# Routing gates of a decoder trunk placed by float32r products of eight columns, as a rounded part and a remainder

## The chip, the cores and the metric

The kernel runs on one core of a Trainium2 chip. A core has the engines TensorE (PE in the profile: matrix products; PEld is its weight load), VectorE (DVE), ScalarE (ACT), GpSimd (POOL) and SyncE (SP, whose queue starts most of the transfers). The metric is the time of one execution in microseconds; it is 798.51 for the kernel before.

## What is computed

The reference is a decoder trunk of two layers over 256 tokens of 1024 numbers in float32. Each layer mixes tokens with three kinds of attention, attends to 256 memory tokens, and ends in a mixture of 16 experts in 4 groups. The change touches only the last. Its gates are, for each token, a weight for two experts of one group:

```python
scores = sigmoid(x @ router_w);  biased = scores + router_bias
g_sel  = argmax over the 4 groups of (sum of the two highest biased scores in the group)
expert_idx = the two highest biased in group g_sel
w = scores[expert_idx];  w = w / sum(w)          # gates, zero for all other experts
hg = x @ w_gate[e];  hu = x @ w_up[e]            # for each expert e: 1024 -> 256
a  = silu(hg) * hu * gates[:, e]
out += a @ w_down[e]                             # 256 -> 1024
```

## The kernel before

**Arithmetic.** Large products are made of halves: each float32 operand is kept as a part rounded to float32r and a remainder, and one product is three float32r products (`product`, L1669 to L1671). ScalarE makes the rounded part of each weight piece (L564), VectorE the remainder (`split_lo`, L570), into a ring of four slots. A piece is 128 partitions by 1024 columns; an expert has four pieces for its gate and up matrices (names `U<e>`) and two for its down matrix (`D<e>`).

**The experts.** Every token goes to one group. Its place in the group's list of up to 128 slots is kept as a matrix `sel` of zeros and ones (tokens by slots, for each of two token tiles `t` and four groups `g`), of type float32r. `gather` multiplies the tokens by `sel`, so that each group's tokens stand in slots (`xg_hi`, `xg_lo`). The 16 experts then run one after another, each on the 128 slots of its group: `experts_up` (four pieces of six products), an activation (`silu` on ScalarE, `act_of` on VectorE, L1390, which also multiplies by the gate `gs[:, e]` of each slot), two transposes (`turn_a`, L1939), and `experts_down`.

**The gates.** On VectorE, `router_first` and `router_gates` work out two weights per token in a row of small operations on the 4 experts of the token's group. Each ends in a semaphore, and the next waits for it (`step`). The last one, L1370, writes `g4`, tokens by the 4 experts of the group, in float32. On TensorE, `place_gates` (L2008 to L2014) brings them to the slots: for each group and token tile, `sel` is the stationary operand and `g4` the moving one, 8 products of 4 columns into columns 0 to 15 of `bank[5]`. VectorE copies them out into `gs` (L1617).

**What sets the order.** Each engine's order is written out by hand. On VectorE it is, after the piece u+4: `router_first`, `router_gates`, `full_group` (three small operations, L1380 to L1385, about groups with more than 128 tokens), the remainders of pieces u+5 and u+6, a wait for `gs_done`, L1617, `act_of` for expert 0, then pieces u+7 and u+8. On TensorE it is, in `expert_turn(l, 0)`: `experts_up` of expert 1 for piece 0 (u+4), `place_gates`, `experts_up` for piece 1 (u+5), `turn_a` of expert 0 (which waits for `act_of`), pieces 2 and 3, and `experts_down` of expert 0. All of this happens once in each of the two layers.

Of the kernel before, what the change touches and what calls it, by code (L numbers as in the profile page):

```python
# [19 lines left out]
F32 = mybir.dt.float32  # L20
F32R = mybir.dt.float32r
I32 = mybir.dt.int32
ALU = mybir.AluOpType
ACT = mybir.ActivationFunctionType
AX = mybir.AxisListType.X

P = 128
# [5 lines left out]
NE, NG, EPG, DE = 16, 4, 4, 256  # L33
# [43 lines left out]
def build(nc, x, mem, positions, w_in, b_forget, mla_q_gain, mla_kv_gain, mla_w_uq, mla_w_ukv, w_mix_out,  # L77
          ln_mix_g, ln_mix_b, xattn_w_q, xattn_w_kv, xattn_w_o, ln_mem_g, ln_mem_b, router_w, router_bias,
          expert_w_gate, expert_w_up, expert_w_down, ln_ffn_g, ln_ffn_b, out):
    _, T, DM = x.shape  # L80
    L = w_in.shape[0]
    TT = T // P
# [60 lines left out]
    with ExitStack() as ctx:  # L143
# [3 lines left out]
        def sb(name, shape, dt=F32, at=None):  # L147
            size = int(np.prod(shape[1:])) * 4
            size = -(-size // 64) * 64
            if at is None:  # L150
                at = place[0]
                place[0] += size
            return nc.alloc_sbuf_tensor_at(name, shape, dt, offset=at), at + size


        raw, _ = sb("raw", [P, RAW, 1024])
        w_split, _ = sb("w_split", [P, 2, SPL, 1024], F32R)
        w_hi, w_lo = w_split[:, 0, :, :], w_split[:, 1, :, :]
        xs, _ = sb("xs", [P, TT, DM])
        xT_at = place[0]  # L160
        xT_hi, _ = sb("xT_hi", [P, KC, T], F32R)
        xT_lo, _ = sb("xT_lo", [P, KC, T], F32R)
        memT_hi, _ = sb("memT_hi", [P, KC, T], F32R)
        memT_lo, _ = sb("memT_lo", [P, KC, T], F32R)
        gb, _ = sb("gb", [P, 2, DM])
        ident, _ = sb("ident", [P, P])

        causal, _ = sb("causal", [P, 2 * P])
        dilmask, _ = sb("dilmask", [P, 2 * P])
        dilcount, _ = sb("dilcount", [P, 2 * P])  # L170
        upto, _ = sb("upto", [P, P], F32R)
# [18 lines left out]
        iota, _ = sb("iota", [P, P])  # L190
        ing_r, _ = sb("ing", [P, TT * NG], F32R)
        ing = ing_r[:, :].bitcast(F32)
        g4, _ = sb("g4", [P, TT, EPG])
        posg, _ = sb("posg", [P, TT, NG])
        pos1, _ = sb("pos1", [P, TT])
        gs, _ = sb("gs", [P, NE])
# [94 lines left out]
        def signal(name, per, ahead=0):  # L291
            return Signal(sem(name), per, ahead)
# [86 lines left out]
        fz_a = signal("fz_a", 2)  # L379
        aug = signal("aug", 2)  # L380
        rope_step = signal("rope_step", 26)
        route = signal("route", 29)
        group_at = 14
        counted_over = signal("counted_over", 3)
        xs_a = signal("xs_a", TT)
# [687 lines left out]
        def _(dve):  # L1073
# [210 lines left out]
            def by_tile(v, n_):  # L1284
                return v[:, 0:TT * n_].rearrange("p (t n) -> p t n", t=TT)
# [71 lines left out]
            def router_gates(l):  # L1357

                step = stepper(l)
                mine, other = by_tile(R[13], EPG).unsqueeze(3).to_broadcast(GRID), by_tile(R[13], EPG).unsqueeze(2).to_broadcast(GRID)  # L1360
                over_, tied, rank = R[4], R[5], G4(R[6])
                step(nc.vector.tensor_tensor(grid(over_), other, mine, ALU.is_gt))
                step(nc.vector.tensor_tensor(grid(tied), other, mine, ALU.is_equal))
                step(nc.vector.tensor_tensor(grid(tied), grid(tied), earlier[:, :, :].unsqueeze(1).to_broadcast(GRID), ALU.mult))
                step(nc.vector.tensor_tensor(over_, over_, tied, ALU.add))
                step(nc.vector.tensor_reduce(by_tile(rank, EPG), grid(over_), AX, ALU.add))
                step(nc.vector.scalar_tensor_tensor(G4(R[7]), rank, 1.5, G4(R[14]), ALU.is_lt, ALU.mult))
                step(nc.vector.tensor_reduce(R[9][:, 0:TT], by_tile(R[7], EPG), AX, ALU.add))
                step(nc.vector.reciprocal(R[9][:, TT:2 * TT], R[9][:, 0:TT]))
                step(nc.vector.tensor_tensor(g4[:, :, :], by_tile(R[7], EPG),  # L1370
                                             R[9][:, TT:2 * TT].unsqueeze(2).to_broadcast([P, TT, EPG]), ALU.mult))
                assert q[0] == route.per, q[0]

            def over_full(l):
# [72 lines left out]
            for l in range(L):  # L1447
# [166 lines left out]
                split_lo(dve, u + 5)  # L1614
                split_lo(dve, u + 6)
                dve.wait_ge(gs_done.sem, gs_done.at(l, 1))
                nc.vector.tensor_copy(gs[:, :], bank[5][:, 0:NE]).then_inc(gs_ready.sem, 1)  # L1617
                dve.wait_ge(gs_ready.sem, gs_ready.at(l, 1))
                act_of(l, 0, 0)
                for i in range(u + 7, u + 9):  # L1620
# [30 lines left out]
        def _(pe):  # L1651
# [39 lines left out]
            def by_tile(l):  # L1691

                open_job(l, "A")
                parts = {}
                for t, b in enumerate(banks(l, "A")):
                    last_half = evac_v[l][job[f"XT{t}"]]
                    pe.wait_ge(job_v.sem, job_v.at(l, last_half - 1))
                    for j in range(4):
                        if t == 0:
                            if j == 2:  # L1700
                                pe.wait_ge(x_in[1], 16)
                                turn_x(l, "XT1", 1, 0)
                            parts[j] = sub_in(index[l, "A", j])
                        if j == 2:
                            pe.wait_ge(job_v.sem, job_v.at(l, last_half))
                        for k in range(2):
                            lhs = tuple(v[:, 2 * j + k, t * P:(t + 1) * P] for v in xT)
                            r = tuple(v[:, k * A_W:(k + 1) * A_W] for v in parts[j])
                            ins = product(b[:, 0:A_W], lhs, r, j == 0 and k == 0, j == 3 and k == 1)
                        if t == TT - 1:  # L1710
                            ins.then_inc(split_free, 1)
# [294 lines left out]
            def place_gates(l):  # L2006

                pe.wait_ge(route.sem, route.at(l, route.per))  # L2008
                for g in range(NG):
                    for t in range(TT):  # L2010
                        ins = nc.tensor.matmul(bank[5][:, g * EPG:(g + 1) * EPG],
                                               sel[:, t, g * P:(g + 1) * P].bitcast(F32), g4[:, t, :],
                                               start=g == 0 and t == 0, stop=g == NG - 1 and t == 1, skip_group_check=True)
                ins.then_inc(gs_done.sem, 1)  # L2014

# [36 lines left out]
            def further_tokens(l):  # L2052
                pe.wait_ge(y_v.sem, y_v.at(l, 2 * NG))
                pe.wait_ge(ov_picked.sem, ov_picked.at(l, 1 + TT))
                pe.nop().then_inc(paused_t, 1)
                for t in range(TT):
                    nc.tensor.transpose(bank[6][:, t * P:(t + 1) * P], ov_sel[:, t, :], ident[:, :])
                for t in range(TT):
                    nc.tensor.matmul(bank[7][:, 0:EPG], ov_sel[:, t, :], g4[:, t, :], start=t == 0, stop=t == 1)
                for f in range(KC):  # L2060
                    for t in range(TT):
                        ins = nc.tensor.matmul(bank[4 + f // 4][:, (f % 4) * P:(f % 4 + 1) * P],
                                               xs[:, t, f * P:(f + 1) * P], ov_sel[:, t, :],
                                               start=f % 4 == 0 and t == 0, stop=t == 1, skip_group_check=True)
                ins.then_inc(ov_gathered.sem, 1)
                pe.wait_ge(ov_kept.sem, ov_kept.at(l, 5))
                pe.nop().then_inc(paused_t, 1)
                with pe.Fori(0, EPG) as e:
                    pe.wait_ge(ov_in[l], e * 48 + 48)
                    for kc in range(KC):  # L2070
                        ins = nc.tensor.matmul(bank[6][:, :], ov_x[:, kc, :], ov_up[:, kc, :], start=kc == 0, stop=kc == KC - 1)
                    ins.then_inc(ov_upped.sem, 1)
                    pe.wait_ge(ov_act.sem, ov_act.at(l, e + 1))
                    for c_ in range(2):
                        ins = nc.tensor.transpose(bank[7][:, c_ * P:(c_ + 1) * P], act_a[:, 0, c_ * P:(c_ + 1) * P], ident[:, :])
                    ins.then_inc(ov_turned.sem, 1)
                    pe.wait_ge(ov_aT_in.sem, ov_aT_in.at(l, e + 1))
                    for c_ in range(2):
                        for h in range(2):
                            ins = nc.tensor.matmul(bank[4 + h][:, :], ov_aT[:, c_, :], ov_down[:, c_, 512 * h:512 * h + 512],  # L2080
                                                   start=c_ == 0, stop=c_ == 1)
                    ins.then_inc(ov_used.sem, 1)
                pe.wait_ge(ov_y_in.sem, ov_y_in.at(l, ov_y_in.per))
                pe.nop().then_inc(paused_t, 1)
                for t in range(TT):
                    for h in range(2):
                        nc.tensor.matmul(bank[2 * t + h][:, :], ov_selT[:, t * P:(t + 1) * P],
                                         ov_y[:, 512 * h:512 * h + 512], start=False, stop=False, skip_group_check=True)
# [203 lines left out]
```

## Time and profile before

| | |
|---|---|
| median of three runs | 798.51 us (797.60 to 798.68) |
| the profiled execution | 800.22 us, its span 798.6 us |
| TensorE matmul busy | 783.0 us, 98% of the span |
| VectorE busy | 620.9 us, 78% |
| ScalarE busy | 512.0 us, 64% |
| mean granted TensorE clock | 0.996 of full |
| transfers | 177.06 MB, 222 GB/s over the span |

The span is the profiled stretch on the core; the execution's own time is 1.62 us longer. Busy time says how long an engine had work, not whether the kernel waited for it; the timeline shows where an engine sat idle and which instruction ended that. In the timeline a row's second number is how long its instructions took from first start to last end, `x16` how many were merged into it, and the brackets hold the idle time before it and what released it. A float32 product stands in the records as two matmuls and two weight loads, so the 8 products of `place_gates` are `x16`; a float32r product stands as one, though its type is printed as f32 too.

### The profile page before, as it was taken

The numbers are of one execution on the slowest core, as the hardware profiler recorded it, in microseconds if no ns is written. First come the engines' busy times: TensorE is split into PE (matmuls) and PEld (weight loads), VectorE is DVE, ScalarE is ACT, GpSimd is POOL, SyncE is SP. The second block draws the span as 40 slices with busy tenths as digits, with TensorE's granted clock in tenths as the row PEclk, the third lists the DMA queues.
The fourth block names the chain that finished last, engine by engine and source line by source line (L and its number), as shares of the span: only waits on it lengthen the run. The fifth ranks groups of instructions, "written<-read, shape, count | busy, mean of one in ns | idle before, by whom it ended". The sixth has DMA issues, their size and how long they took to land.

```text
span 798.6 us, 11973 instructions
## 1 busy us (share of the span) xinstructions
PE 783.0 (98%) x4307; PEld 676.7 (85%) x4307; DVE 620.9 (78%) x1066; ACT 512.0 (64%) x794; POOL 79.3 (10%) x150
## 2 busy tenths in 40 slices
PE   7999999999999999999999999999999999999995
PEld 7999997789888888888899998878998788888884
DVE  4767867685669999999884578777655899999995
ACT  4755556454547788888755566565443768888873
POOL 3259100020000000000011233002000000000000
PEclk9999999999999999999999999999999999999998
DMA  9965343564345699999956544445633359999951
GB/s 326 319 201 177 135 134 124 164 234 142 106 150 164 225 365 369 367 364 368 361 142 205 157 159 132 133 158 185 199 112 116 133 168 359 368 364 367 368 192 54
DMA packets 123118, 177.06 MB, mean 222 GB/s; under 512 B 10176, under 2 KB 92624, under 8 KB 123056
## 3 DMA queue, kind: packets, MB, share of 16 engines
q1 hardware_dynamic: 121072, 169.56, 63.6%
q0 software_dynamic: 1984, 6.70, 2.8%
q8 instruction: 36, 0.59, 0.3%
q14 instruction: 26, 0.21, 0.1%
HBM read 175.18 MB, written 1.05 MB: 221 GB/s over the span
## 4 chain that ended last, share of the span: by engine, by line
PE 88%; DVE 8%; issue 1%; ACT 1%; DMA 1%; DVEq 0%; SPq 0%; ACTq 0%
PE bank L1669 24%; PE bank L1671 24%; PE bank L1670 24%; DVE w_split L570 2%; PE bank L1876 2%; PE bank L1919 2%; PE bank L1910 2%; PE bank L1889 2%; DVE xg_lo L1605 1%; PE bank L1845 1%; PE bank L1865 1%; PE bank L1939 1%; PE bank L1782 1%; DVE xs L1208 1%; PE bank L2024 1%
## 5 line engine op out<-in xcount | busy, mean ns | idle before, releaser
L570 DVE TENSOR_TENSOR w_split<-raw,w_split 128x1024 fp32r<-128x1024 f32 (+3 forms) x334 | 385.4, 1176 | 93.3 <-ACT w_split L564 88.6
L564 ACT ACTIVATE w_split<-raw 128x1024 fp32r<-128x1024 f32 (+3 forms) x334 | 334.8, 1010 | 108.5 <-PE bank L1671 95.1
L1669 PE MATMUL bank<-w_split,xg_hi 128*128 128x512 f32 x256 | 103.0, 402 | 0.1
L1671 PE MATMUL bank<-w_split,xg_lo 128*128 128x512 f32 x256 | 100.2, 391 | 0.0
L1670 PE MATMUL bank<-w_split,xg_hi 128*128 128x512 f32 x256 | 99.9, 390 | 0.0
L1669 PE MATMUL bank<-w_split,xT_hi 128*128 128x384 f32 (+2 forms) x224 | 78.6, 351 | 1.9 <-DVE xT_lo L1135 1.9
L1671 PE MATMUL bank<-w_split,xT_lo 128*128 128x384 f32 (+2 forms) x224 | 76.5, 342 | 0.0
L1670 PE MATMUL bank<-w_split,xT_hi 128*128 128x384 f32 (+2 forms) x224 | 76.4, 341 | 0.0
L1671 PEld LDWEIGHTS bank<-w_split,xg_lo 128*128 128x128 f32 x256 | 48.0, 188 | 10.3
L1669 PEld LDWEIGHTS bank<-w_split,xg_hi 128*128 128x128 f32 x256 | 48.1, 188 | 9.6 <-DVE xg_lo L1605 0.6
L1670 PEld LDWEIGHTS bank<-w_split,xg_hi 128*128 128x128 f32 x256 | 48.2, 188 | 9.0
L1669 PE MATMUL bank<-w_split,mixT_hi 128*128 128x512 f32 x128 | 51.8, 405 | 0.1
L1671 PE MATMUL bank<-w_split,mixT_lo 128*128 128x512 f32 x128 | 50.0, 391 | 0.0
L1670 PE MATMUL bank<-w_split,mixT_hi 128*128 128x512 f32 x128 | 50.0, 390 | 0.0
L1671 PE MATMUL bank<-w_split,aT_lo 128*128 128x512 f32 x128 | 49.8, 389 | 0.0
L1669 PE MATMUL bank<-w_split,aT_hi 128*128 128x512 f32 x128 | 49.8, 389 | 0.0
L1670 PE MATMUL bank<-w_split,aT_hi 128*128 128x512 f32 x128 | 49.8, 389 | 0.0
L1669 PEld LDWEIGHTS bank<-w_split,xT_hi 128*128 128x128 f32 x224 | 42.6, 190 | 2.7 <-DVE xT_lo L1135 2.3
L1670 PEld LDWEIGHTS bank<-w_split,xT_hi 128*128 128x128 f32 x224 | 42.8, 191 | 0.2
L1671 PEld LDWEIGHTS bank<-w_split,xT_lo 128*128 128x128 f32 x224 | 42.6, 190 | 0.1
L794 ACT ACTIVATE qkT<-bank 66x512 f32<-66x512 f32 (+2 forms) x26 | 15.5, 596 | 33.2 <-PE bank L1845 27.0
L1669 PE MATMUL bank<-xT_hi,w_split 128*128 128x256 f32 x112 | 32.4, 289 | 0.0
(325 smaller groups left out, 1514.3 us busy)
## 6 DMA issues: line engine op xcount, KB each, us to landing
raw<-in_expert_w_gate_dram SPq DMA_DIRECT2D x128, 256.0 KB, 6.0
raw<-in_expert_w_up_dram SPq DMA_DIRECT2D x128, 256.0 KB, 7.6
raw<-in_expert_w_down_dram SPq DMA_DIRECT2D x64, 512.0 KB, 7.8
raw<-in_xattn_w_kv_dram SPq DMA_DIRECT2D x32, 512.0 KB, 3.7
raw<-in_w_in_dram SPq DMA_DIRECT2D x40, 384.0 KB, 4.9
raw<-in_w_mix_out_dram SPq DMA_DIRECT2D x16, 512.0 KB, 3.4
raw<-in_xattn_w_q_dram SPq DMA_DIRECT2D x16, 512.0 KB, 3.4
raw<-in_xattn_w_o_dram SPq DMA_DIRECT2D x16, 512.0 KB, 5.2
```

Source lines behind the costliest of these rows:

```text
L564: nc.scalar.activation(halves_of(i)[0][:, 0:w], raw[:, i % RAW, 0:w], ACT.Copy).then_inc(hi_ready, 1)
L570: nc.vector.tensor_tensor(lo[:, 0:w], raw[:, i % RAW, 0:w], hi[:, 0:w].bitcast(F32), ALU.subtract).then_inc(lo_ready, 1)
L794: nc.scalar.activation(qkT[0:d, qk_slot(h), :], B_QK[0:d, :], ACT.Copy).then_inc(qkT_ready.sem, n)
L1208: nc.vector.scalar_tensor_tensor(half, half, ALPHA, product, ALU.mult, ALU.add, accum_out=st[:, 2 * n_ + t, 2 * h:2 * h + 1]).then_inc(sig ...
L1605: nc.vector.tensor_tensor(xg_lo[:, f, :, :].rearrange("p g s -> p (g s)"), bank[XG_BANKS[f]][:, :], xg_hi[:, f, :, :].rearrange("p g s -> ...
L1669: nc.tensor.matmul(o, lhs[0], rhs[0], start=first, stop=False, skip_group_check=shared)
L1670: nc.tensor.matmul(o, lhs[0], rhs[1], start=False, stop=False, skip_group_check=shared)
L1671: return nc.tensor.matmul(o, lhs[1], rhs[0], start=False, stop=last, skip_group_check=shared)
L1876: ins = nc.tensor.matmul(o[:, t * T:(t + 1) * T], qTx[:, 2 * g + c_, t * P:(t + 1) * P], kTx[:, 2 * g + c_, :], start=c_ == 0, stop=c_ == 1)
L1889: ins = nc.tensor.transpose(B_PT[:, k * P:(k + 1) * P], pr[:, k * P:(k + 1) * P], ident[:, :])
L1910: ins = nc.tensor.matmul(B_O[k * HD:(k + 1) * HD, q0:T], v[:, t, g - 1 + k, :], turned_of(h - 1 + k)[:, t * T:t * P + T], start=t == 0, st ...
L1919: ins = nc.tensor.matmul(value_bank(h)[:, dblk * T:(dblk + 1) * T], vx[:, c_, f * P:(f + 1) * P], turned_of(h)[:, c_ * T:(c_ + 1) * T], st ...
```

## The change

`g4` becomes `g_parts` of type float32r, with two halves for each tile: the gates rounded to float32r, and what the rounding left out. L1370 writes the first half, and a new step of two operations (one for each token tile, with the reciprocal as a per-partition scalar) works out the product again and subtracts the first half from it. `place_gates` multiplies by both halves at once: 8 products of 8 columns, both operands float32r, into columns 0 to 31 of `bank[5]`. On the way out a sum over pairs replaces the copy. `route` counts 31 instead of 29 steps. The rest of the diff is in `further_tokens`, a branch that is taken only where a group has more than 128 tokens.

```diff
-        g4, _ = sb("g4", [P, TT, EPG])
+        g_parts, _ = sb("g_parts", [P, TT, 2, EPG], F32R)
...
-        route = signal("route", 29)
+        route = signal("route", 31)
...
-                step(nc.vector.tensor_tensor(g4[:, :, :], by_tile(R[7], EPG),
+                step(nc.vector.tensor_tensor(g_parts[:, :, 0, :], by_tile(R[7], EPG),
                                              R[9][:, TT:2 * TT].unsqueeze(2).to_broadcast([P, TT, EPG]), ALU.mult))
+                step(*(nc.vector.scalar_tensor_tensor(g_parts[:, t, 1, :], by_tile(R[7], EPG)[:, t, :],
+                                                      R[9][:, TT + t:TT + t + 1], g_parts[:, t, 0, :].bitcast(F32),
+                                                      ALU.mult, ALU.subtract) for t in range(TT)))
...
                 dve.wait_ge(gs_done.sem, gs_done.at(l, 1))
-                nc.vector.tensor_copy(gs[:, :], bank[5][:, 0:NE]).then_inc(gs_ready.sem, 1)
+                nc.vector.tensor_reduce(gs[:, :].rearrange("p (g e) -> p g e", g=NG),
+                                        bank[5][:, 0:2 * NE].rearrange("p (g s e) -> p g e s", g=NG, s=2), AX, ALU.add)\
+                    .then_inc(gs_ready.sem, 1)
...
-                        ins = nc.tensor.matmul(bank[5][:, g * EPG:(g + 1) * EPG],
-                                               sel[:, t, g * P:(g + 1) * P].bitcast(F32), g4[:, t, :],
+                        ins = nc.tensor.matmul(bank[5][:, 2 * g * EPG:2 * (g + 1) * EPG],
+                                               sel[:, t, g * P:(g + 1) * P], g_parts[:, t, :, :].rearrange("p s e -> p (s e)"),
                                                start=g == 0 and t == 0, stop=g == NG - 1 and t == 1, skip_group_check=True)
```

The order on VectorE from the end of the router's steps to the first activation, before. `rt` is the router's scratch, `g_82` is `g4`, `fl` belongs to `full_group`, and `w_split` is the ring of weight pieces (here u+5 and u+6).

```order
L1369 RECIPROCAL rt<-rt 128x2
L1370 TENSOR_TENSOR g_82<-rt 128x8
L1380 SCALAR_TENSOR_TENSOR fl<-iota,fl 128x4
L1382 TENSOR_REDUCE fl<-fl 128x2
L1385 CAST flag<-fl 1x2
L570 TENSOR_TENSOR w_split<-raw,w_split 128x1024 x2
L1617 COPY gs<-bank 128x16
L1390 SCALAR_TENSOR_TENSOR act_a<-silu,gs,bank 128x256
```

The same place in the changed kernel.

```order
L1369 RECIPROCAL rt<-rt 128x2
L1370 TENSOR_TENSOR g_parts<-rt 128x2x4
L1372 SCALAR_TENSOR_TENSOR g_parts<-rt,g_parts 128x4 x2
L1383 SCALAR_TENSOR_TENSOR fl<-iota,fl 128x4
L1385 TENSOR_REDUCE fl<-fl 128x2
L1388 CAST flag<-fl 1x2
L570 TENSOR_TENSOR w_split<-raw,w_split 128x1024 x2
L1620 TENSOR_REDUCE gs<-bank 128x16
L1393 SCALAR_TENSOR_TENSOR act_a<-silu,gs,bank 128x256
```

Two operations are new, in front of `full_group` and the two weight pieces, and the copy has become a reduction; nothing else on this engine has moved.

On TensorE, before: the last products of expert 1's piece 0, `place_gates`, and the first of its piece 1.

```order
L1670 MATMUL bank<-w_split,xg_hi 128x512
L1671 MATMUL bank<-w_split,xg_lo 128x512
L2011 MATMUL bank<-g_82,sel 128x4 x8
L1669 MATMUL bank<-w_split,xg_hi 128x512
L1670 MATMUL bank<-w_split,xg_hi 128x512
```

The same place in the changed kernel.

```order
L1675 MATMUL bank<-w_split,xg_hi 128x512
L1676 MATMUL bank<-w_split,xg_lo 128x512
L2016 MATMUL bank<-g_parts,sel 128x8 x8
L1674 MATMUL bank<-w_split,xg_hi 128x512
L1675 MATMUL bank<-w_split,xg_hi 128x512
```

The eight products stay where they were; their moving operand has eight columns in place of four.

## Rows read from the trace of the kernel before

**Rows 1.** The page: the chain that ended last, by engine.
```profile
PE 88%; DVE 8%; issue 1%; ACT 1%; DMA 1%; DVEq 0%; SPq 0%; ACTq 0%
```

**Rows 2.** Timeline, VectorE, layer 0: start us, us, engine, line, work [idle before <-releaser].
```profile
265.17 0.17 DVE L1370 TENSOR_TENSOR g<-rt 128x8 f32<-128x8 f32 x1
265.61 0.16 DVE L1380 SCALAR_TENSOR_TENSOR fl<-iota,fl 128x4 f32<-128x4 f32 x1 [0.27 <-DVE g L1370]
...
266.07 0.16 DVE L1385 CAST flag<-fl 1x2 int32<-1x2 f32 x1
266.15 2.34 DVE L570 TENSOR_TENSOR w_split<-raw,w_split 128x1024 fp32r<-128x1024 f32 x2
268.42 0.15 DVE L1617 COPY gs<-bank 128x16 f32<-128x16 f32 x1
268.61 0.48 DVE L1390 SCALAR_TENSOR_TENSOR act_a<-silu,gs,bank 128x256 f32<-128x256 f32 x1
```

**Rows 3.** Timeline, TensorE's weight loads in the same stretch of layer 0.
```profile
265.39 1.86 PEld L2011 LDWEIGHTS bank<-g,sel 128*128 128x128 f32 x16 [0.23 <-DVE g L1370]
267.41 0.19 PEld L1669 LDWEIGHTS bank<-w_split,xg_hi 128*128 128x128 f32 x1 [0.16 <-DVE w_split L570]
...
269.14 0.20 PEld L1939 LDWEIGHTS bank<-ident,act_a 128*128 128x128 f32 x2 [0.51 <-DVE act_a L1390]
```

**Rows 4.** Timeline, the same place in layer 1: VectorE.
```profile
651.24 0.17 DVE L1370 TENSOR_TENSOR g<-rt 128x8 f32<-128x8 f32 x1
651.44 0.16 DVE L1380 SCALAR_TENSOR_TENSOR fl<-iota,fl 128x4 f32<-128x4 f32 x1
...
654.44 0.48 DVE L1390 SCALAR_TENSOR_TENSOR act_a<-silu,gs,bank 128x256 f32<-128x256 f32 x1
```

**Rows 5.** Timeline, the same place in layer 1: TensorE's weight loads.
```profile
651.45 1.86 PEld L2011 LDWEIGHTS bank<-g,sel 128*128 128x128 f32 x16 [0.22 <-DVE g L1370]
653.24 0.19 PEld L1669 LDWEIGHTS bank<-w_split,xg_hi 128*128 128x128 f32 x1
...
654.97 0.20 PEld L1939 LDWEIGHTS bank<-ident,act_a 128*128 128x128 f32 x2 [0.51 <-DVE act_a L1390]
```

**Rows 6.** Stage table: us, busy time (instructions) of each engine, granted clock, DMA.
```profile
core 0: us, PE busy (x) PEld busy (x) DVE busy (x) ACT busy (x) POOL busy (x), PEclk, DMA share, GB/s
265.39:269.34 3.95, 3.80 (x26) 3.11 (x25) 3.56 (x8) 1.35 (x2) 0.00 (x0) 1.00 0.36 103
269.34:300.00 30.66, 30.66 (x140) 25.24 (x139) 29.30 (x30) 25.12 (x29) 0.00 (x0) 1.00 1.04 349
788.00:792.00 4.00, 1.28 (x6) 0.74 (x4) 3.77 (x13) 1.63 (x4) 0.00 (x0) 1.00 0.00 0
792.00:796.00 4.00, 0.00 (x0) 0.00 (x0) 3.93 (x5) 1.45 (x3) 0.00 (x0) 0.60 0.32 131
```

**Rows 7.** Timeline, VectorE, an earlier place where two small operations share one wait.
```profile
247.06 0.17 DVE L1319 TENSOR_TENSOR rt<-rt 128x16 f32<-128x16 f32 x1
247.16 0.17 DVE L1320 TENSOR_TENSOR rt<-rt 128x16 f32<-128x16 f32 x1
247.36 0.17 DVE L1321 TENSOR_TENSOR rt<-rt 128x8 f32<-128x8 f32 x1
```

**Rows 8.** VectorE operations by line: count, ns min/median/max, first to last start.
```profile
L1355 DVE TENSOR_REDUCE rt<-rt x4: 209/210/211, 262.7 to 649.3; 128x8 f32<-128x32 f32 x4
...
L1366 DVE TENSOR_REDUCE rt<-rt x2: 186/186/186, 264.3 to 650.4; 128x8 f32<-128x32 f32 x2
...
L1214 DVE TENSOR_SCALAR st<-st x12: 214/214/214, 163.6 to 791.7; 128x1 f32<-128x1 f32 x12
```

**Rows 9.** Timeline, TensorE: the ranking products, with float32r operands and four columns.
```profile
248.86 0.27 PE L1975 MATMUL bank<-ing,upto 128*128 128x4 f32 x1 [0.27 <-DVE ing L1330]
...
249.21 0.36 PE L1980 MATMUL bank<-ing,ones 128*128 128x4 f32 x2
249.44 0.48 PE L1812 MATMUL bank<-memT_hi,ones 128*128 128x512 f32 x1
```

More of the change, by code:

```diff
@@ L2058, in further_tokens @@
                 for t in range(TT):
-                    nc.tensor.matmul(bank[7][:, 0:EPG], ov_sel[:, t, :], g4[:, t, :], start=t == 0, stop=t == 1)
+                    for s_ in range(2):
+                        nc.tensor.matmul(bank[7][:, 0:EPG], ov_sel[:, t, :], g_parts[:, t, s_, :].bitcast(F32),
+                                         start=t == 0 and s_ == 0, stop=t == 1 and s_ == 1)
                 for f in range(KC):
```

## Prediction

> **What bounds the kernel now.** I read the chain that ended last first: 88% of it lies on TensorE and 8% on VectorE [rows 1]. So time taken off TensorE is worth something wherever TensorE is not waiting, and time put on VectorE costs nothing wherever VectorE is ahead. The question is which of the two holds at the one place per layer that is edited. For that I read the timeline of both engines around line 1370, in each layer.
>
> In layer 0 VectorE ends the gates at 265.17 + 0.17 = 265.34, and TensorE's first weight load of the placing starts at 265.39, after 0.23 us in which it sat idle for L1370 [rows 2, 3]. The reader is to see that TensorE is already the one that waits. The placing's 16 loads take 1.86 us. The next product, of piece u+5, starts at 267.41; the bracket gives 0.16 us of idle time and names the remainder L570 as what ended it [rows 3]. VectorE did that remainder right behind `full_group`: two in a row from 266.15, 2.34 us for both, so the first ends at about 267.3 [rows 2]. Then VectorE goes on without a gap: second remainder, copy of the gates at 268.42, activation at 268.61 for 0.48 us. TensorE's transposes start at 269.14 after 0.51 us of waiting for that activation [rows 2, 3].
>
> So between 265.17 and 269.14 every start on VectorE follows from its own instruction before, and TensorE waits for it three times. The copy never waited for the products: the placing ends before 267.41, and the copy stands in VectorE's queue at 268.42 behind the two remainders. Layer 1 is the same to a few hundredths: 0.22 us of waiting at the placing, the activation at 654.44, 0.51 us of waiting at 654.97 [rows 4, 5]. Only at piece u+5 no idle time is shown there: at 653.24 placing and remainder end together [rows 5].
>
> Behind this place it is the other way round. From 269.34 to 300 TensorE is busy 30.66 of 30.66 us and VectorE 29.30 [rows 6]. A TensorE that starts that stretch later ends it later; nothing there takes a delay back. Transfers are not tied to the clock on the wall either: their buffers come free by these same engines, so they move along.
>
> **The change, part by part.**
>
> First, two operations on VectorE in front of `full_group`. They share one wait. Where two small operations already do that, the first starts at 247.06, the second at 247.16 and the next step at 247.36: such a step is 0.30 us long [rows 7]. A step of one is 0.20 us, L1370 to L1380 in layer 1 [rows 4]. The new step is added whole, so +0.30 us in front of `full_group`, of both remainders, the copy and the activation, and also in front of the placing, which now waits for 31 steps. Below, it can't be less than one step, 0.20 us. Above: the new operations take a scalar from each partition, and a tiny operation that does (L1214) is recorded at 0.214 us against some 0.16 to 0.17 for those without [rows 8, 2]; with that and no overlap within the pair it is 0.21 + 0.25 = 0.46 us. I take 0.30, since the pair is the nearest row.
>
> The Trainium skill says on this, in "VectorE: DVE Perf Modes", section "Terms", that the pipe is drained after each operation and that the next can't issue before. Read strictly, the pair would stand end to end, 0.17 + 0.20 = 0.37 us; by that the sum below would be 0.8 in place of 0.7. The trace doesn't bear the strict reading out: the second starts 0.10 us after the first, whose record is 0.17 long [rows 7].
>
> Second, the reduction in place of the copy. The copy is 0.15 us [rows 2]. Reductions that read 32 numbers per partition take 0.186 us with the summed ones side by side and 0.210 us with a stride of four [rows 8]; the new one reads 32 with a stride of four, from `bank[5]`, and writes 16. I take +0.04 us; the bounds are 0 and, since no row has a reduction out of a bank, twice the larger difference, 0.11 us. It stands straight in front of the activation, so all of it is on the path.
>
> Third, the placing on TensorE. The records have 16 loads in 1.86 us; with 0.19 for one load that is 1.67/15 = 0.11 us from start to start [rows 3]. Products with float32r operands are one load and one matmul each, and go at the same pace: five of them from 248.86 to 249.44, 0.116 us each [rows 9]. That they have four columns and the new ones eight hardly counts, because the load sets the pace. So the placing shrinks from about 1.86 to 8 x 0.116 = 0.93 us, 0.93 us less per layer. Its worth: TensorE would be done at 265.69 + 0.93 = 266.62, but the remainder of u+5 now comes at 267.41 + 0.30 = 267.71. The idle 0.16 us becomes 1.09 us. The saving turns into waiting and buys nothing; nor does the earlier `gs_done`, since VectorE gets to it only at 268.72.
>
> Then nothing else is late: the transposes start at 269.14 + 0.34 = 269.48, still behind the activation, with about the same 0.5 us of waiting, since the products of u+5 and the activation are both moved by 0.30 and 0.34 us. The transposed remainders, pieces u+7 to u+9 and the products after them keep their distances.
>
> Sum per layer: 0.30 + 0.04 = 0.34 us. Two layers: +0.68 us. The span goes from 798.6 to 799.3, the profiled execution from 800.22 to 800.9. The median of the runs lies 1.71 us under that execution; with the same distance it goes from 798.51 to 799.2 us.
>
> One thing can shift this by tenths. In layer 0 VectorE starts L1380 0.44 us after L1370, in layer 1 0.20 us [rows 2, 4]; the extra 0.24 us has no cause in the profile. A program with other instructions in front of that place may have such a pause in neither layer or in both: -0.24 or +0.24. With it, the bounds of the sum are 2 x 0.20 - 0.24 = 0.2 us and 2 x (0.46 + 0.11) + 0.24 = 1.4 us, so 798.7 to 799.9, and with the spread of the runs shown (0.9 below the median to 0.2 above) 797.8 to 800.1.
>
> **The rivals.**
>
> *TensorE is what ends the stretch.* Then halving the placing pays. For it: the chain is 88% TensorE [rows 1], and in layer 1 the profile shows no idle time in front of 653.24 [rows 5]. Against it: in both layers TensorE waits 0.51 us for the activation afterwards, and would wait longer if it came earlier. If all of it paid and VectorE's part were hidden, 2 x 0.93 = 1.9 us less: 796.7 us. If the saving paid and the additions too counted, 1.2 us less: 797.3, which can't be told from no change.
>
> *The additions are hidden.* If a later place had room for 0.34 us, the time would stay at 798.5. For it, TensorE waits for VectorE, ScalarE and transposed tiles here and there outside the experts. Against it, each of these waits hangs on work that moves along with the delay.
>
> *The clock falls.* This one is slower. The wait in front of u+5 grows to 1.1 us, with another 0.5 us only 1.5 us later. If that made the granted clock fall to 1.2 GHz for the products behind it, they would take twice as long. An expert is 36 products and two transposes; at 30.66/140 = 0.22 us each [rows 6] that is 8.3 us. For half an expert at the lower level I put 4.2 us: one layer gives 803.4 us, both 807.6. It decides if any stretch behind 267 or 653 shows less than 1.00. Against it stands the end of the program: from 788 to 792 TensorE is busy 1.28 of 4 us and the clock is still 1.00; it reads 0.60 only in the next four, in which TensorE does nothing [rows 6]. The Trainium skill warns of this in "TensorE: Matmul & The Clock Gate", section "Why this matters for your kernels": idle gaps between bursts of matmuls bring the clock back to the half rate. As far as these rows show it, a gap of 1.1 us among busy microseconds is not such a gap.
>
> *The change doesn't do what it says.* If the eight-column products were run in two passes like float32 ones, the placing would stay at 1.9 us and end at 265.69 + 1.86 = 267.55, still before 267.71. The time would be the forecast's, 799.2; only the reason for the missing gain would differ.
>
> **How the numbers follow.** The forecast, +0.7 us with its bounds and with the case of two passes inside it, gets 0.76. Hidden additions 0.12, TensorE as the bound 0.07 (half of it at 796.7), a falling clock 0.05. About 0.2%, 1.6 us, is what a measurement of this kernel can tell from no change: below 796.9 is faster, above 800.1 slower. Faster comes from the rival at 796.7 alone, 0.04. Slower is the falling clock and a little of the forecast's upper bound, 0.08. The rest, 0.88, is no change. The range is 797.4 to 800.4 us.
>
> **What the changed profile would show.** The placing as eight loads in about 0.9 us. Idle time of 1 us or more on TensorE in front of the next L1669's counterpart, ended by the remainder. From the start of L1370 to the start of the first activation 3.78 us in layer 0, where it was 3.44, and 3.54 in layer 1, where it was 3.20. A wait near 0.5 us in front of the transposes. Clock 1.00 throughout. The forecast is wrong if TensorE's wait for the activation shrinks well below 0.5 us or is gone, which would mean that VectorE was not what ended the stretch, or if the added step measures far from 0.30 us.

## The result and the profile after

The changed kernel takes 799.82 us (799.28 to 800.91, 18 runs) against 798.69 (797.40 to 800.17, 18 runs) for the one before. The ratio is 1.0017, interval 1.0010 to 1.0024: 0.8 to 1.9 us slower. The ratio lies inside the 0.2% that the prediction calls no change, the upper end of its interval just outside. The same comparison made again (same_after, below) gave 1.0024 (1.0014 to 1.0034). The forecast was +0.7 us, so direction and class were right and 799.82 lies in the range of 797.4 to 800.4; the size was about half of what was measured.

The chain that ended last, on the page of the profile after, has one hundredth more of VectorE than [rows 1]:

```profile
PE 88%; DVE 9%; issue 1%; ACT 1%; DMA 1%; DVEq 0%; SPq 0%; ACTq 0%
```

VectorE in layer 0, from the timeline, against [rows 2]:

```profile
263.70 0.17 DVE L1370 TENSOR_TENSOR g_parts<-rt 128x8 fp32r<-128x8 f32 x1
263.91 0.36 DVE L1372 SCALAR_TENSOR_TENSOR g_parts<-rt,g_parts 128x4 fp32r<-128x4 f32 x2
264.30 0.16 DVE L1383 SCALAR_TENSOR_TENSOR fl<-iota,fl 128x4 f32<-128x4 f32 x1
...
264.83 2.34 DVE L570 TENSOR_TENSOR w_split<-raw,w_split 128x1024 fp32r<-128x1024 f32 x2
267.10 0.17 DVE L1620 TENSOR_REDUCE gs<-bank 128x16 f32<-128x32 f32 x1
267.31 0.48 DVE L1393 SCALAR_TENSOR_TENSOR act_a<-silu,gs,bank 128x256 f32<-128x256 f32 x1
```

TensorE's weight loads there, against [rows 3]:

```profile
264.32 0.97 PEld L2016 LDWEIGHTS bank<-g_parts,sel 128*128 128x128 f32 x8 [0.61 <-DVE g_parts L1372]
266.09 0.19 PEld L1674 LDWEIGHTS bank<-w_split,xg_hi 128*128 128x128 f32 x1 [0.81 <-DVE w_split L570]
...
267.85 0.20 PEld L1944 LDWEIGHTS bank<-ident,act_a 128*128 128x128 f32 x2 [0.53 <-DVE act_a L1393]
```

And layer 1, against [rows 4, 5], first VectorE, then the weight loads:

```profile
649.93 0.17 DVE L1370 TENSOR_TENSOR g_parts<-rt 128x8 fp32r<-128x8 f32 x1
...
650.52 0.16 DVE L1383 SCALAR_TENSOR_TENSOR fl<-iota,fl 128x4 f32<-128x4 f32 x1
...
653.53 0.48 DVE L1393 SCALAR_TENSOR_TENSOR act_a<-silu,gs,bank 128x256 f32<-128x256 f32 x1
```

```profile
652.32 0.19 PEld L1674 LDWEIGHTS bank<-w_split,xg_hi 128*128 128x128 f32 x1 [0.81 <-DVE w_split L570]
```

What to see: the placing halves, 1.86 to 0.97 us, and TensorE then waits 0.81 us for the remainder of piece u+5, where it waited 0.16 or not at all. (The prediction had 1 us or more here for layer 0; the pause of 0.24 us, which went, makes up most of the difference.) The transposes still wait 0.53 us. From L1370 to the activation it is 3.61 us in layer 0 (3.44 before, 3.78 forecast) and 3.60 in layer 1 (3.20 before, 3.54 forecast). From there on the two profiles agree: activation 0 to L1370 of layer 1 is 382.62 us against 382.63, the activation of layer 1 to the last entry of the chain 141.03 against 141.01. So this profile holds +0.57 us. Its span is still 0.9 us shorter than the span before, because it reached L1370 1.47 us sooner; and the starts of profiles differ by up to 2.8 us from one to another (below). Comparing two spans would have given the wrong sign.

### The profile page after: what moved, and what is told of

Same layout as the page of the kernel before. It is cut to its first block, busy times and chain, and to the rows that moved or that the text cites. A ratio compares the mean times of both kernels' runs of the same rounds, so it can differ in the third digit from the quotient of the medians.

```text
span 797.7 us, 11945 instructions
## 1 busy us (share of the span) xinstructions
PE 780.1 (98%) x4291; PEld 673.5 (84%) x4291; DVE 621.6 (78%) x1070; ACT 511.7 (64%) x794; POOL 79.4 (10%) x150
## 3 DMA queue, kind: packets, MB, share of 16 engines
HBM read 175.18 MB, written 1.05 MB: 221 GB/s over the span
## 4 chain that ended last, share of the span: by engine, by line
PE 88%; DVE 9%; issue 1%; ACT 1%; DMA 1%; DVEq 0%; SPq 0%; ACTq 0%
PE bank L1674 24%; PE bank L1676 24%; PE bank L1675 24%; DVE w_split L570 2%; PE bank L1881 2%; PE bank L1924 2%; PE bank L1915 2%; PE bank L1894 2%; DVE xg_lo L1608 1%; PE bank L1850 1%; PE bank L1870 1%; PE bank L1944 1%; DVE xs L1208 1%; PE bank L1787 1%; PE bank L2029 1%
```

## The experiments

All were timed beside the kernel before, whose median was 798.6 to 798.8 us each time. Three stretches of each profile, in us, from starts on VectorE and the start of the chain's last entry:

| | L1370 to activation, layer 0 | the same, layer 1 | activation of layer 1 to the chain's last entry | time, ratio (interval) |
|---|---|---|---|---|
| same_before | 3.44 | 3.20 | 141.01 | 798.62, 1.0003 (0.9994 to 1.0011) |
| same_after | 3.61 | 3.60 | 142.31 | 800.40, 1.0024 (1.0014 to 1.0034) |
| tensor_part | 3.44 | 3.20 | 141.01 | 798.61, 1.0002 (0.9993 to 1.0011) |
| vector_part | 3.59 | 3.59 | 143.23 | 805.85, 1.0097 (1.0082 to 1.0111) |
| vector_part_b | 3.59 | 3.59 | 141.00 | 799.54, 1.0014 (1.0004 to 1.0024) |
| after_placed_twice | 3.61 | 3.61 | 142.38 | 799.63, 1.0014 (1.0005 to 1.0023) |
| after_wide_filler | 3.61 | 3.61 | 141.01 | 799.24, 1.0001 (0.9992 to 1.0010) |
| late_before | 2.91 | 2.67 | 141.45 | 798.18, 0.9994 (0.9985 to 1.0003) |
| late_after | 3.09 | 3.08 | 141.04 | 798.56, 0.9997 (0.9988 to 1.0006) |
| moved_64 | 3.44 | 3.20 | 143.19 | 805.10, 1.0080 (1.0067 to 1.0092) |
| reordered_before | 2.60 | 2.58 | 140.97 | 799.22, 1.0005 (0.9996 to 1.0014) |
| reordered_after | 1.95 | 1.96 | 140.79 | 797.71, 0.9984 (0.9975 to 0.9992) |

L1354 first started at 262.5 us in the first profile before, at 259.8 in tensor_part's and at 259.7 in after_placed_twice's: that is how far the starts differ. In the two reordered kernels one remainder has moved in front of L1370, so their first two columns can't be held against the other rows; the text on them uses another start.

**same_before and same_after: the two kernels again.**

> The kernel before, unchanged, against itself: what a comparison of this kernel with no change gives, and how far two profiles of it lie apart. All theories: ratio 1.000 within 0.1%. From the start of L1370 to the activation 3.2 us in layer 1; in layer 0 3.44 us if the pause of 0.24 us is fixed to this program, 3.20 us if it comes and goes by itself.

The pause of 0.24 us in layer 0 is in every profile that keeps this order without the step (and in late_before), and in none with the step: it belongs to the program, not to chance.

> The changed kernel again, on the same chip as the parts. Theory A: the sum of the two parts, +0.6 to +0.8 us, ratio 1.001; both layers 3.6 us from L1370 to the activation. If the 1.3 us measured before hold here while vector_part gives 0.7 and tensor_part 0, something other than the two parts costs 0.6 us.

Slower than the parts allow. The activation is where it should be, but the stretch behind it is 1.3 us longer, 142.31. Its timeline, TensorE:

```profile
654.28 0.78 PE L1674 MATMUL bank<-w_split,xg_hi 128*128 128x512 f32 x1
654.85 0.63 PE L1675 MATMUL bank<-w_split,xg_hi 128*128 128x512 f32 x1
655.28 0.63 PE L1676 MATMUL bank<-w_split,xg_lo 128*128 128x512 f32 x1
655.71 0.63 PE L1674 MATMUL bank<-w_split,xg_hi 128*128 128x512 f32 x1
656.13 0.63 PE L1675 MATMUL bank<-w_split,xg_hi 128*128 128x512 f32 x1
656.56 0.52 PE L1676 MATMUL bank<-w_split,xg_lo 128*128 128x512 f32 x1
656.92 0.40 PE L1674 MATMUL bank<-w_split,xg_hi 128*128 128x512 f32 x1
657.15 0.40 PE L1675 MATMUL bank<-w_split,xg_hi 128*128 128x512 f32 x1
```

A product every 0.43 us in place of 0.23: the lower of the two clock levels. Its stage table says the same (the third figure from the end is the granted clock, as a share of full; half is the lower level):

```profile
650.00:660.00 10.00, 9.09 (x37) 7.03 (x37) 8.99 (x15) 4.91 (x7) 0.00 (x0) 0.83 0.67 211
```

Another fall of this kind stands near the start of most profiles, whatever the kernel. The stage from 9 to 13 us in same_before, then in same_after:

```profile
9.00:13.00 4.00, 4.00 (x16) 3.29 (x15) 2.62 (x3) 1.69 (x2) 0.00 (x0) 0.57 1.05 396
9.00:13.00 4.00, 4.00 (x20) 3.82 (x19) 2.71 (x3) 1.33 (x2) 0.00 (x0) 1.00 1.06 398
```

Nine of the fourteen profiles show it, between 8 and 15 us; before, tensor_part, late_before, same_after and after_placed_twice don't. This matters below.

**tensor_part: only the placing in one pass.** The gates are rounded to float32r and the remainder is left out of the computation.

```diff
-        g4, _ = sb("g4", [P, TT, EPG])
+        g4, _ = sb("g4", [P, TT, EPG], F32R)
...
-                                               sel[:, t, g * P:(g + 1) * P].bitcast(F32), g4[:, t, :],
+                                               sel[:, t, g * P:(g + 1) * P], g4[:, t, :],
```

> The kernel before, with only the placing in one pass: the gates are rounded to float32r and the remainder is left out of the computation, 8 products of 4 columns, copy as before. Theory A: TensorE is free 0.9 us earlier and waits as much longer for the remainder of piece u+5 (about 0.9 to 1.0 us of idle time in layer 0, 0.8 in layer 1); time +0.0 us, ratio 1.000. Rival (TensorE sets the end): up to -1.9 us, ratio 0.998. Theory B: +0.5 us or more, with a lower granted clock behind 267 or 653.

Nothing gained, all stretches as before. Weight loads in layer 0:

```profile
262.68 0.97 PEld L2011 LDWEIGHTS bank<-g,sel 128*128 128x128 f32 x8 [0.23 <-DVE g L1370]
264.70 0.19 PEld L1669 LDWEIGHTS bank<-w_split,xg_hi 128*128 128x128 f32 x1 [1.05 <-DVE w_split L570]
```

The 0.89 us saved stand in the next bracket: 0.16 became 1.05. The rival that TensorE ends this stretch is refuted.

**vector_part: only the step, into a spare tile.**

```diff
+        g_lo, _ = sb("g_lo", [P, TT, EPG], F32R)
...
-        route = signal("route", 29)
+        route = signal("route", 31)
...
+                for _ in range(1):
+                    step(*(nc.vector.scalar_tensor_tensor(g_lo[:, t, :], by_tile(R[7], EPG)[:, t, :],
+                                                          R[9][:, TT + t:TT + t + 1], g4[:, t, :],
+                                                          ALU.mult, ALU.subtract) for t in range(TT)))
```

> The kernel before, with only the added step of two operations on VectorE (its result is written to a spare tile that nothing reads); placing in float32 with four columns and copy as before. Theory A (VectorE sets the end of this place, all of the cost is its added step): the step takes 0.39 us from start to start, L1370 to the activation 3.6 us in both layers, time +0.6 to +0.8 us, ratio 1.001, as in the changed kernel. Theory B (the longer wait of TensorE costs something of its own): less than half of that, 0.3 us or below is left, as TensorE's work is not shortened here.

The step shows as expected, but 7.2 us came with it, spread over the program. The spare tile had moved all later tiles by 64 bytes. That spoiled the experiment; two more took it apart. (The change itself moves nothing: `g_parts` fills the 64 bytes that were set aside for `g4`.)

**vector_part_b: the step without the move.** The changed kernel with placing and copy as before; the remainder is worked out but left out of the result.

```diff
-                nc.vector.tensor_reduce(gs[:, :].rearrange("p (g e) -> p g e", g=NG),
-                                        bank[5][:, 0:2 * NE].rearrange("p (g s e) -> p g e s", g=NG, s=2), AX, ALU.add)\
-                    .then_inc(gs_ready.sem, 1)
+                nc.vector.tensor_copy(gs[:, :], bank[5][:, 0:NE]).then_inc(gs_ready.sem, 1)
...
-                        ins = nc.tensor.matmul(bank[5][:, 2 * g * EPG:2 * (g + 1) * EPG],
-                                               sel[:, t, g * P:(g + 1) * P], g_parts[:, t, :, :].rearrange("p s e -> p (s e)"),
+                        ins = nc.tensor.matmul(bank[5][:, g * EPG:(g + 1) * EPG],
+                                               sel[:, t, g * P:(g + 1) * P].bitcast(F32), g_parts[:, t, 0, :].bitcast(F32),
```

> The changed kernel with its VectorE step kept and everything else undone: placing in float32 with four columns of the rounded part (the remainder is left out of the result), copy in place of the reduction; all tiles lie where they lie in the changed kernel. Theory A (the added VectorE step is all of the cost): as same_after, +1.1 to +1.7 us, ratio 1.0014 to 1.0024. Theory B (the step costs 0.17 and 0.40 us, and the rest of the 1.1 to 1.7 us comes from the longer wait of TensorE, behind which the clock falls in some executions): here TensorE's placing takes its old 1.9 us and the wait for piece u+5 is short, so +0.6 us, ratio 1.0007, no clock below 1.00 behind 267 or 653. If the 7 us of vector_part come back, they belong to the step; if not, to the 64 bytes by which its spare tile moved the others.

The 7 us are gone, and the step alone gives 1.0014: the lower edge of theory A's figures, with an interval that holds theory B's too. So it is the VectorE step that costs, not the placing. Its single profile has no fall of the clock at 653 and no long wait at u+5, but it is one of the nine with the fall near the start, and no profile has both. Whether all of the cost is the step's own length this profile doesn't tell; its single executions say more (below).

**moved_64: the move without the step.**

```diff
+        spare, _ = sb("spare", [P, 16])
```

> The kernel before with one unused tile of 64 bytes behind g4, so that all later tiles lie 64 bytes higher; no instruction is added. If place in memory is what cost vector_part its 7 us: +6 to +7 us, ratio 1.008 to 1.009, spread over the products of TensorE (their mean at 512 columns 395 ns in place of 390). If not, 0.

6.3 us for an unused tile. The groups by line, first of same_before, then of moved_64 (duration in ns, min/median/max; in moved_64 the same product is one line lower):

```profile
L1670 PE MATMUL bank<-w_split,xg_hi x256: 387/389/397, 256.4 to 773.9; 128*128 128x512 f32 x128
...
L1670 PE MATMUL bank<-w_split,mixT_hi x128: 387/389/402, 136.9 to 622.1; 128*128 128x512 f32 x128
L1670 PEld LDWEIGHTS bank<-w_split,aT_hi x128: 187/188/188, 270.8 to 782.1; 128*128 128x128 f32 x128
L1670 PE MATMUL bank<-w_split,aT_hi x128: 389/389/389, 271.1 to 782.3; 128*128 128x512 f32 x128
```

```profile
L1671 PE MATMUL bank<-w_split,xg_hi x256: 391/396/398, 257.1 to 779.8; 128*128 128x512 f32 x128
...
L1671 PE MATMUL bank<-w_split,mixT_hi x128: 392/394/398, 136.8 to 625.9; 128*128 128x512 f32 x128
L1671 PEld LDWEIGHTS bank<-w_split,aT_hi x128: 187/188/188, 271.5 to 788.1; 128*128 128x128 f32 x128
L1671 PE MATMUL bank<-w_split,aT_hi x128: 387/389/395, 271.8 to 788.4; 128*128 128x512 f32 x128
```

The medians of products whose stationary operand lies behind the spare tile (`xg`, `mixT`) are 5 to 7 ns longer; that of `aT`, in front of it, has not moved. By the means of all groups of 512 columns, the 768 products with `xg` take 4.9 ns more each (394.5 to 399.4) and the 384 with `mixT` 4.4 (395.3 to 399.7), in sum 5.5 us; the 384 with `aT` take 1.6 ns more (389.0 to 390.6), which adds 0.6.

**after_placed_twice: TensorE kept at work, narrow products.**

```diff
-                for g in range(NG):
+                for g in [g for _ in range(2) for g in range(NG)]:
```

> The changed kernel, but TensorE does the eight products of the placing twice, so that it works through the 0.9 us in which it would wait for piece u+5. Theory A: TensorE isn't what ends this place; the time is that of same_after, ratio 1.0014 to 1.0024. Theory B: more work on TensorE makes it faster: the wait is gone and with it the lower clock in some executions; 0.5 to 0.8 us less than same_after, ratio 1.0007. If TensorE set the end, 1.9 us more.

Not the recovery of theory B, though its figure of 1.0007 lies inside the interval. The wait at u+5 is filled, and the clock fell all the same; the loads take 0.33 us instead of 0.19 from 652.95 on, and the stage table reads half:

```profile
649.14 1.86 PEld L2016 LDWEIGHTS bank<-g_parts,sel 128*128 128x128 f32 x16 [0.56 <-DVE g_parts L1372]
650.92 0.19 PEld L1674 LDWEIGHTS bank<-w_split,xg_hi 128*128 128x128 f32 x1
...
652.67 0.29 PEld L1944 LDWEIGHTS bank<-ident,act_a 128*128 128x128 f32 x2 [0.52 <-DVE act_a L1393]
652.95 0.33 PEld L1674 LDWEIGHTS bank<-w_split,xg_hi 128*128 128x128 f32 x1
```

```profile
653.00:655.00 2.00, 2.00 (x7) 1.61 (x6) 2.00 (x3) 1.33 (x2) 0.00 (x0) 0.50 0.87 275
```

So the fall doesn't need the wait at u+5; and 0.9 us of extra TensorE work cost nothing.

**after_wide_filler: the same time filled with products of 512 columns.**

```diff
                 ins.then_inc(gs_done.sem, 1)
+                for _ in range(4):
+                    nc.tensor.matmul(bank[3][:, :], ones[:, :], memT_hi[:, 0:2, :].rearrange("p k t -> p (k t)"),
+                                     start=True, stop=True)
```

> The changed kernel with four products of 512 columns (0.9 us, into a bank that nothing reads then) behind the placing, in the wait for piece u+5. In same_after and after_placed_twice, but in no profile without the VectorE step, the clock fell to 1.2 GHz for 3.4 us at 653 and cost 1.3 us. Theory C (the stretch without wide products, from the end of expert 1's piece 0 to piece u+5, brings it about, and narrow products don't end it): the fall is gone, clock 1.00 behind 267 and 653; the time is before plus the steps alone, +0.6 us, ratio 1.0007, and single executions as low as 798.0 us appear. Theory D (the falls have to do with something else): as same_after and vector_part_b, +0.9 to +1.8 us.

The stretches are as long as in same_after without its fall, and five of eleven executions lie at 797.95 to 798.26 us. Of 53 executions of after, same_after, vector_part_b and after_placed_twice only one was that low. The clock of the profile reads 1.00 here:

```profile
650.00:660.00 10.00, 9.78 (x47) 7.56 (x47) 9.72 (x16) 6.24 (x9) 0.00 (x0) 1.00 0.72 195
```

That row alone would prove little, since this profile too has the fall near the start. The single executions are the evidence, by their mean granted clock. In the fourteen profiles it is 0.993 or 0.994 where one of the two falls stands, and 0.996 where neither does. So a mean of 0.995 or more marks an execution that escaped both. (Near the limit that is rough, since the third decimal can move by other things; with 0.996 as the limit the first two rows below are 25 of 93 and 3 of 53.) Counted so:

| | executions that escaped both falls |
|---|---|
| before, beside all experiments | 40 of 93 |
| after, same_after, vector_part_b, after_placed_twice | 4 of 53 |
| after_wide_filler | 5 of 11, all at 0.997 and all of them its low ones |

Five of the 53 read 0.992 or less and none of the 93, so some seem to have both falls. vector_part doesn't fit: it has the step, and four of its five executions read 0.995 or more; its tiles lie 64 bytes further on.

**late_before, late_after: `full_group` out of the way.**

```diff
                 router_gates(l)
-                full_group(l)
                 split_lo(dve, u + 5)
...
                     expert_turn(l, e, e // EPG - 1 if e % EPG == 0 else None)
+                    if e == 3:
+                        full_group(l)
```

> The kernel before, with the three operations of full_group moved from in front of piece u+5 to behind expert 3, where nothing waits for them. Both theories: VectorE reaches u+5 0.8 to 1.0 us earlier; TensorE then is bound by its own placing and products and reaches the transposes 0.2 us (layer 1) to 0.5 us (layer 0) earlier; time -0.7 us, ratio 0.999.

> The changed kernel with full_group behind expert 3. L1370 to the activation 2.8 us in place of 3.6; the wait in front of u+5 falls from 0.8 to 0.3 us or less. Theory A: 2 x 0.4 us less than same_after, about the time of before, ratio 1.0005 to 1.001. Theory B: that and the clock's share, ratio 1.000 or a little below. Neither gives more than late_before, since VectorE's longer chain still ends last.

VectorE reached the activation 0.5 us sooner in each layer. In late_before's profile most of it was given back in layer 1 (141.45 against 141.01), with a wait that the profile before doesn't have:

```profile
688.95 0.19 PEld L1670 LDWEIGHTS bank<-w_split,aT_hi 128*128 128x128 f32 x1 [0.39 <-DVE aT_lo L1395]
```

That wait comes 8 us after the three operations (680.37 to 680.98). Whether they caused it isn't shown: they stand at the same place in layer 0 and in both layers of late_after, where nothing is given back.

late_before's median is 0.4 us below before, with an interval that holds 1; late_after stands level with before. With VectorE relieved the change's cost is within the noise.

**reordered_before, reordered_after: an order in which the placing counts.** Beside `full_group` late, the remainder of u+5 goes in front of the router's steps, the placing behind the products of u+5, and the transposes behind the products of one more piece:

```diff
                 split_lo(dve, u + 4)
+                split_lo(dve, u + 5)
                 router_first(l)
                 router_gates(l)
-                full_group(l)
-                split_lo(dve, u + 5)
...
+                if e == 0:
+                    experts_up(l, e + 1, (0, 1))
+                    place_gates(l)
+                    experts_up(l, e + 1, (2,))
+                    turn_a(l, e, e % 2)
+                    experts_up(l, e + 1, (3,))
+                    experts_down(l, e)
+                    return
                 experts_up(l, e + 1, (0,))
-                if e == 0:
-                    place_gates(l)
                 experts_up(l, e + 1, (1,))
```

> The kernel before with full_group late, the remainder of piece u+5 in front of the router's steps, and the placing behind the products of u+5; TensorE then has no wait at piece u+5 and the placing counts. Against before: idle time of 0.7 to 0.9 us per layer falls to some 0.2, so -0.3 to -1.2 us, ratio 0.9985 to 0.9996.

> The changed kernel in the same new order. Here the shorter placing is on the path, and the added step of 0.39 us has TensorE's products of u+5 beside it: 2 x 0.9 us less than its own order would cost with the long placing, and as a bound 2 x 0.5 us less than reordered_before; against before -1.0 to -2.0 us, ratio 0.9975 to 0.9988. If it isn't below reordered_before, VectorE still sets the end and the change doesn't pay in this order either.

reordered_after is faster than both kernels: 797.71 us, 0.9984 (0.9975 to 0.9992). In this order VectorE waits for the long placing, as its rows in reordered_before show (first), and not for the short one, in reordered_after (second):

```profile
264.80 1.22 DVE L570 TENSOR_TENSOR w_split<-raw,w_split 128x1024 fp32r<-128x1024 f32 x1
266.99 0.17 DVE L1616 COPY gs<-bank 128x16 f32<-128x16 f32 x1 [0.96 <-PE bank L2018]
```

```profile
265.38 1.22 DVE L570 TENSOR_TENSOR w_split<-raw,w_split 128x1024 fp32r<-128x1024 f32 x1
266.52 0.18 DVE L1619 TENSOR_REDUCE gs<-bank 128x16 f32<-128x32 f32 x1
```

Between the two kernels of this order the change is worth 1.5 us of 799 by the medians. reordered_before missed its range. A start that all orders share shows why: from the start of the last four remainders of the gathered tokens (L1605, in the changed kernel L1608) to the activation it is 9.63 and 9.39 us in the two layers of same_before, 9.92 and 9.89 in reordered_before, 9.28 and 9.28 in reordered_after. So with the long placing VectorE reached the activation 0.3 and 0.5 us later than in the old order, with the short one 0.35 and 0.1 us sooner. Both new kernels gained another 0.24 and 0.28 us from the activation of layer 0 to that start in layer 1 (376.36 us in same_before).

## Why the prediction was right, and where it fell short

**VectorE sets this place; the placing's saving turns into waiting.** Shown in this order by tensor_part (ratio 1.0002, 0.89 us saved and 0.89 us waited) and by after_placed_twice, where twice the placing moves nothing. The transposes wait 0.53 us, as forecast.

**The added step.** Put at 0.30 us, it measures 0.39 (263.91 to 264.30, 650.13 to 650.52). The two operations are longer than those that I went by:

```profile
L1372 DVE SCALAR_TENSOR_TENSOR g_parts<-rt,g_parts x4: 216/220/223, 263.9 to 650.3; 128x4 fp32r<-128x4 f32 x4
```

Each is 0.22 us, near the 0.214 of L1214 in my upper bound, where the pair of [rows 7] has 0.17. They take 0.36 us together, so the second starts about 0.14 us after the first, and the next step 0.25 us after that. The row I went by has neither a per-partition scalar nor a float32r result; which of these makes the difference was not tried. The strict reading of the pipe's drain in the Trainium skill ("VectorE: DVE Perf Modes", "Terms") came nearer with 0.37, but by luck: the pair doesn't stand end to end here either, it overlaps by some 0.08 us.

**The reduction.** 0.21 us to the activation's start in place of 0.19, so +0.02 where I had +0.04.

**The pause in layer 0.** It went, as the lower bound allowed, and took 0.24 us off: +0.17 us in layer 0, +0.40 in layer 1, in sum 0.57 us against a forecast of 0.68.

**The falling clock.** This is the step that failed. The sum had nothing for it: I kept it as a rival with a chance of 0.05, arguing from [rows 6] that a gap of 1.1 us was no such gap. The 0.57 us of longer steps alone would have made the forecast good; what came on top, about as much again, is in good part this, as far as the single executions show.

The clock fell at 653 in same_after and after_placed_twice, two of five profiles with the added step in this order and no wide products behind it, and in none of the nine others. Each fall cost 1.3 to 1.4 us (142.31 and 142.38 against 141.01), a third of my price per layer, and it was never seen in layer 0. The two are also the only ones of the five without the fall near the start. So the change takes away the executions that escape the clock's fall: 40 of 93 did before, 4 of 53 with the added step. As an estimate from these counts, some 0.35 to 0.45 falls more per execution, the upper figure with those at 0.992 or less, at 1.3 us each make 0.5 to 0.6 us; with the limit at 0.996 it is 0.3 to 0.4. With the 0.57 us that is 0.8 to 1.2 us, against 1.13 by the medians and 0.8 to 1.9 by the interval. The falls seem to be there in vector_part_b too, with 2 of 11, whose only profile couldn't show it.

My account of it as a matter of the idle gap was wrong as well. tensor_part had the gap of 1.05 us without the step, and 6 of its 12 executions escaped both falls, as many as before. Filling the gap with narrow products left the fall, filling it with wide ones brought the low executions back. What decides in which executions the clock falls stays open, and so does why most of vector_part's executions escaped.

**Two passes.** Refuted: eight loads, 0.97 us.

## What to carry to other kernels

When a step gets shorter, read the bracket of the next wait first: if another engine ends it, the saving is only moved there, and the work added on that other engine is the price. The price can be larger than its length: here the granted clock fell in more executions, which one profile before and one after didn't show, and the mean clock of the single executions did. The same change can pay once the order is such that the shortened engine is the one waited for; here it took putting one piece ahead of the router's steps, the placing and the transposes later, and three operations off the chain. When kernels are compared, or a spare tile is added for an experiment, keep every tile's address: 64 bytes moved the time ten times as far as the change's steps did.

## What was not expected of the hardware

An unused tile of 64 bytes in front of the work area cost 6.3 us (1.0067 to 1.0092): products with 512 columns whose stationary operand was moved took 4.4 to 4.9 ns more on average, while their weight loads stayed at 188 ns. The sizes in front of that area add up to 140,288 bytes, a multiple of 512, which the tile undid; which alignment matters was not tried.

With products of 8 columns in the wait for u+5 the granted clock fell to half at 653 (after_placed_twice), and 1 of 12 executions escaped both falls; with four products of 512 columns there it was 5 of 11 (after_wide_filler).
